# A gated attention / gMLP decoder layer: 18 projection column tiles, taken in pairs, by a seven-product scheme over two thirds of the tokens

## The reference, cut to what matters

```python
h = _rmsnorm(x, g_mp)
z = h @ w_in                    # columns: q | k | v (768 each) | u (512) | v_sg (512) | gate_a | gate_b
o_a, rows = core(q, k, v)       # dilated window attention, 3 groups x 4 heads; rows: k and v to keep
vs = _layernorm(jax.nn.gelu(vs), lvg, lvb)
o_b = jax.nn.gelu(u) * _spatial_mix(vs, w_sg, b_sg)      # chunks of 128 tokens
m = jax.nn.sigmoid(ga) * (o_a @ w_pa) + jax.nn.sigmoid(gb) * (o_b @ w_pb)
x = x + _rmsnorm(m @ w_o, g_mq)
h = _rmsnorm(x, g_fp)
x = x + _rmsnorm((jax.nn.silu(h @ w_g) * (h @ w_u)) @ w_d, g_fq)
```

## Time and profile before

| | |
|---|---|
| median of 3 runs | 1502.27 us (1501.37 to 1504.39) |
| span of the profiled execution | 1499.6 us, its own time is not listed apart |
| PE busy | 1480.6 us, 99% of the span |
| DVE, ACT, POOL busy | 49%, 40%, 14% |
| granted PE clock | 0.997 of full speed over the span |
| DMA | 147 MB, 98 GB/s in the mean |

### The profile page before, as it was taken

How to read it: one execution, slowest core, us unless ns; L and a number is a source line. 1 busy time by engine, 2 the same in 40 slices (tenths; PEclk the granted TensorE clock), 3 DMA queues, 4 the chain that set the end, 5 groups by cost and what they waited for, 6 DMA issues and landing times.

```text
span 1499.6 us, 26632 instructions
## 1 busy us (share of the span) xinstructions
PE 1480.6 (99%) x11001; PEld 1433.9 (96%) x11001; DVE 733.7 (49%) x1328; ACT 595.6 (40%) x1183; POOL 216.0 (14%) x225
## 2 busy tenths in 40 slices
PE   7999999999999999999999999999999999999998
PEld 6999999999999999997789999999999999999997
DVE  6104552242213437474678857655755683225323
ACT  6215553443224522245586333333333363235322
POOL 2000000000000026150003224222422210002000
PEclk9999999999999999999999999999999999999999
DMA  5111113111112127125644222232232474446341
GB/s 198 47 52 43 43 30 103 29 30 32 53 43 75 30 85 211 46 86 171 231 128 145 71 86 92 72 100 85 79 99 86 138 243 132 114 111 196 113 141 58
DMA packets 186666, 147.09 MB, mean 98 GB/s; under 512 B 7003, under 2 KB 168803, under 8 KB 186549
## 3 DMA queue, kind: packets, MB, share of 16 engines
q1 hardware_dynamic: 182656, 133.31, 29.6%
q0 software_dynamic: 2720, 7.89, 1.8%
q10 hardware_dynamic: 1172, 4.23, 0.7%
HBM read 121.84 MB, written 23.58 MB: 97 GB/s over the span
## 4 chain that ended last, share of the span: by engine, by line
PE 91%; DVE 4%; DMA 2%; ACT 1%; issue 1%; POOL 0%; DVEq 0%; ACTq 0%
PE bank L787 9%; PE bank L789 8%; PE bank L788 8%; PE bank L1357 6%; PE bank L1358 6%; PE bank L1359 6%; PE psAB L1285 3%; PE bank L1285 3%; PE psAB L1287 3%; PE psAB L1286 3%; PE bank L1286 3%; PE bank L1287 3%; PE bankC L787 3%; PE bankC L789 3%; PE bankC L788 3%; PE psT L783 3%
## 5 line engine op out<-in xcount | busy, mean ns | idle before, releaser
L787 PE MATMUL bank<-h_hi,w_hi 128*128 128x344 f32 x752 | 248.6, 331 | 2.7 <-DVE h_lo L2001 2.2
L789 PE MATMUL bank<-h_hi,w_lo 128*128 128x344 f32 x752 | 240.8, 320 | 0.0
L788 PE MATMUL bank<-h_lo,w_hi 128*128 128x344 f32 x752 | 240.5, 320 | 0.0
L1357 PE MATMUL bank<-a_hi,s_hi 128*128 128x258 f32 x704 | 200.2, 284 | 0.2 <-DVE s_lo L2442 0.2
L1358 PE MATMUL bank<-a_lo,s_hi 128*128 128x258 f32 x704 | 198.7, 282 | 0.0
L1359 PE MATMUL bank<-a_hi,s_lo 128*128 128x258 f32 x704 | 198.7, 282 | 0.0
L1988 DVE TENSOR_TENSOR w_lo<-w_raw,w_hi 128x1024 fp32r<-128x1024 f32 x71 | 87.5, 1233 | 203.5 <-ACT w_hi L1398 141.7
L787 PEld LDWEIGHTS bank<-h_hi,w_hi 128*128 128x128 f32 x752 | 142.0, 189 | 7.2 <-issue 3.5
L788 PEld LDWEIGHTS bank<-h_lo,w_hi 128*128 128x128 f32 x752 | 141.9, 189 | 0.0
L789 PEld LDWEIGHTS bank<-h_hi,w_lo 128*128 128x128 f32 x752 | 141.8, 189 | 0.0
L1357 PEld LDWEIGHTS bank<-a_hi,s_hi 128*128 128x128 f32 x704 | 133.0, 189 | 0.6 <-issue 0.5
(11 more groups left out here) (527 smaller groups left out, 3672.6 us busy)
## 6 DMA issues: line engine op xcount, KB each, us to landing
rawd<-in_w_down SPq DMA_DIRECT2D x32, 704.0 KB, 6.5
w_raw<-in_w_in SPq DMA_DIRECT2D x42, 512.0 KB, 3.9
raw<-in_w_gate SPq DMA_DIRECT2D x26, 512.0 KB, 4.1
raw<-in_w_up SPq DMA_DIRECT2D x26, 512.0 KB, 5.3
w_raw<-in_w_out SPq DMA_DIRECT2D x24, 512.0 KB, 3.7
a_raw<-a_rows SPq DMA_DIRECT2D x20, 516.0 KB, 6.2
a_rows<-ab SPq DMA_DIRECT2D x18, 516.0 KB, 2.7
xin<-in_x_prompt SPq DMA_DIRECT2D x8, 512.0 KB, 7.5
```

The source lines that it names most:

```text
L787: mm(out[:, 0:TG], w_hi[par][:, ws], hi[:, k, tgc[tg]], start=first, stop=False)
L788: mm(out[:, 0:TG], w_hi[par][:, ws], lo[:, k, tgc[tg]], start=False, stop=False)
L789: return mm(out[:, 0:TG], w_lo[par][:, ws], hi[:, k, tgc[tg]], start=False, stop=last)
L1357: mm(out, hi[:, k, :], xh[:, k, :], start=(kg == 0 and k == 0), stop=False)
```

## The change

Eighteen of the 26 column tiles of u, v_sg, q, k, v are no longer made as units. Nine *steps* (`SX = 9`) each make two column tiles `e = 0, 1`. Steps 0 to 2 make six tiles of u and v_sg; steps 3 to 8 make the twelve tiles of k and v, those of both head pairs. The two tiles and the two halves of the 1024 input channels form a 2x2 block of weights, and token groups 0 and 1 with the two channel halves form a 2x2 block of activations; their product is made with seven half-depth products (`A11`, `S2`, `A12`, `S3`, `S1`, `A22`, `S4`) in place of eight. Token group 2 is made plainly (`t0` to `t3`). Each is 4 chunks x 3 = 12 matmuls of 344 columns, so a step is 132 matmuls. The two remaining `uv` units stay, and q stays: stages `q0` and `q1` have 3 units each.

Around it:

- **Sums of activations**, once, before step 0: S1, S2, S4 on DVE (seven operations of 128x1376), S3 on POOL (three), and a split of each (ACT, DVE).
- **Sums of weights**: four POOL operations of 128x512 in each step.
- **Splits**: eight slots of 128x512 for each step, four buffered. Slot q + 4 is split once PE is done with slot q, which reads the place that q + 4 takes.
- **Copies out**: four by ACT and five sums by DVE (`u2`, `u3`, `C22`, `C21`, `C12`, 128x344) in each step; PE goes on in a bank after its copy or sum.
- **DRAM**: the k and v tiles go through `stage` to `kv_rows`, six transfers for each step, and are loaded back before their use, pair 0 after the last step and pair 1 in `gb0` and `q1`.
- **The chain of a chunk** is now tied to slots. With i the slot number counted from step 3, chunk c is turned after slot 5c, its statistics stand at 5c + 1, square root, scaling and the next Gelus at 5c + 2, mixing after slot 5c + 3, gating at 5c + 4.
- The `merge` of pair 0 and the turns of pair 1's k and v stand beside 3 units of `q1` in place of 9.

```diff
-STAGES = [("uv", 8, 8), ("qkv0", 9, 9), ("pb", 4, 8), ("gb0", 4, 4), ("qkv1", 9, 9), ("gb1", 4, 4),
+STAGES = [("uv", 2, 2), ("q0", 3, 3), ("pb", 4, 8), ("gb0", 4, 4), ("q1", 3, 3), ("gb1", 4, 4),
+SX = 9
+SX_UV = 3
+SX_TILES = [(0, 6), (0, 7), (0, 8), (0, 3), (0, 4), (0, 5), (1, 4), (1, 5), (1, 3), (1, 6), (1, 7), (1, 8)]
+SX_GROUPS = (("A11", "t0"), ("S2",), ("A12", "t1"), ("S3",), ("t2",), ("S1",), ("A22",), ("S4", "t3"))
+SX_SLOTS = 4
...
@@ tensor
+            def sx_group(s, o, name):
...
+                if s == 0:
+                    if name == "A11":
+                        pe.wait_ge(free[2], 2)
...
+                    if name[0] == "S":
+                        pe.wait_ge(x_lo, 9 + ("S2", "S1", "S3", "S4").index(name) + 1)
...
+                if name == "A12":
+                    pe.wait_ge(lu_s, sx_act(s, "p1"))
+                elif name in ("S3", "A22", "S4"):
+                    pe.wait_ge(sum_s, sx_dve(s, {"S3": "u2", "A22": "u3", "S4": "C22"}[name]))
...
+                for k in range(4):
+                    mm(out, hi[:, k, :], xh[:, k, :], start=(begin and k == 0), stop=False, skip_group_check=True)
+                    mm(out, hi[:, k, :], xl[:, k, :], start=False, stop=False, skip_group_check=True)
+                    ins = mm(out, lo[:, k, :], xh[:, k, :], start=False, stop=(k == 3), skip_group_check=True)
+                ins.then_inc(pe_ev, 1)
...
-            for j in range(9):
-                u, m = U0["qkv0"] + j, M0["qkv0"] + j
-
-                def after(b, tg, j=j):
-                    if tg == 0:
-                        ln_turn(j)
-                    if tg == 2:
-                        ln_mixing(j)
-                unit(u, m, u % 2, 8, h_hi, h_lo, after=after)
+            for s in range(SX):
+                for o in range(8):
+                    pe.wait_ge(sp_lo, 8 * s + o + 1)
+                    for name in SX_GROUPS[o]:
+                        sx_group(s, o, name)
+                    if s >= SX_UV:
+                        c, phase = divmod(8 * (s - SX_UV) + o, 5)
+                        if c < 9 and phase == 0:
+                            ln_turn(c)
+                        elif c < 9 and phase == 3:
+                            ln_mixing(c)
+            pe.wait_ge(lu_s, sx_act(SX - 1, "P1"))
+            pe.wait_ge(sum_s, sx_dve(SX - 1, "C12"))
@@ scalar
+            def sx_high(q):
...
+                if q >= SX_SLOTS:
+                    act.wait_ge(pe_ev, sx_used(q - SX_SLOTS))
...
+                fn(sx_hi[q % SX_SLOTS][:, :, :], sx_source(q), ACT.Copy).then_inc(sp_hi, 1)
...
+                    if s >= SX_UV and c < 9 and phase == 2:
+                        ln_root(c)
+                    sx_high(8 * s + o + SX_SLOTS)
+                    if o == 2:
+                        sx_copy(s, "P0")
+                    elif o == 7:
+                        sx_copy(s, "P1")
@@ vector
+            for name in ("S1", "S2", "S4"):
+                sa_sum(name)
+            sa_low(0, "S2")
+            sx_low(0)
+            sx_low(1)
+            sa_low(1, "S1")
+            sx_low(2)
+            sx_low(3)
+            sa_low(2, "S3")
+            sa_low(3, "S4")
...
+            for s in range(SX):
+                for o in range(8):
+                    if o in (1, 3, 5, 6):
+                        sx_sum(s, {1: "u2", 3: "u3", 5: "C22", 6: "C21"}[o])
+                    sx_low(8 * s + o + SX_SLOTS)
+                    if o == 7:
+                        sx_sum(s, "C12")
+                    if s >= SX_UV:
+                        c, phase = divmod(8 * (s - SX_UV) + o, 5)
+                        if phase == 0 and 1 <= c <= 9:
+                            ob_low(c - 1)
+                        elif c < 9 and phase == 1:
+                            ln_stats(c)
+                        elif c < 9 and phase == 2:
+                            ln_scale(c)
+                        elif c < 9 and phase == 4:
+                            ln_gate(c)
@@ gpsimd
+            sx_weights(0)
+            sa_third()
...
+            sx_in_place(0)
+            for s in range(1, SX):
+                sx_weights(s)
+                sx_in_place(s)
```

More of the change, by code:

```diff
@@ L53, with sx_done, sx_used, sx_act @@
 UNITS, JOBS = _u, _m
+SX = 9
[3 more added lines that the diff above has]
+SX_SLOTS = 4
+SX_SPLITS = 8 * SX
+SX_SUMS, SX_COPIES, SX_EVENTS = 5 * SX, 4 * SX, 11 * SX
+SX_ACT_STEPS = [(s, e) for s in range(SX_UV, SX) for e in range(2)]
+SX_OUT = (64 * (SX - SX_UV), 32 * (SX - SX_UV))
+A_BEFORE = (96, 224, 0, 0, 0, 0)
+SX_FLAT = [x for group in SX_GROUPS for x in group]
+def sx_done(s, what):
+    return len(SX_FLAT) * s + SX_FLAT.index(what) + 1
+def sx_used(q):
+    return sx_done(q // 8, SX_GROUPS[q % 8][-1])
+def sx_act(s, what):
+    return 4 * s + ("p1", "C11", "P0", "P1").index(what) + 1
+def sx_dve(s, what):
+    return 5 * s + ("u2", "u3", "C22", "C21", "C12").index(what) + 1
+def sx_tile(s, e):
+    return 2 * (s - SX_UV) + e
+def sx_by_residue(s):
+    return s >= SX_UV and SX_TILES[sx_tile(s, 0)][1] in (1, 2, 4, 5)
 ORDER = (0, 1, 2, 3, 8, 4, 5, 6, 7)
@@ L865, in kv_turns @@
             def kv_turns(pair, places):
-                last = max(min(p // 2 + 6, 8) for p in places)
-                for tg in range(3):
-                    pe.wait_ge(free[tg], M0[f"qkv{pair}"] + last + 2)
+                pe.wait_ge(a_in[0], 48 * (pair + 1))
+                if max(places) >= 6:
+                    pe.wait_ge(a_in[1], 112 * (pair + 1))
                 if pair:
@@ new lines, in sx_sum @@
+            def sx_sum(s, what):
+                group, e, tg, other = {"u2": ("S2", 1, 0, "p1"), "u3": ("S3", 1, 1, "p1"), "C22": ("S1", 1, 1, "u3"),
+                                       "C21": ("A22", 0, 1, "p1"), "C12": ("S4", 1, 0, "u2")}[what]
+                dve.wait_ge(pe_ev, sx_done(s, group))
+                if other == "p1":
+                    dve.wait_ge(lu_s, sx_act(s, "p1"))
+                else:
+                    dve.wait_ge(sum_s, sx_dve(s, other))
+                if what == "C21":
+                    dve.wait_ge(sum_s, sx_dve(s, "u3"))
+                if s > SX_UV and what in ("u2", "u3"):
+                    late = (e, tg) == (1, 0)
+                    dve.wait_ge(a_out[late], (64, 32)[late] * (s - SX_UV))
+                place = sx_to(s, e, tg)
+                in1 = sx_to(s, 0, 1) if other == "p1" else place
+                v.tensor_tensor(place, sx_from(s, sx_bank(group), tg), in1, ALU.add).then_inc(sum_s, 1)
```

439 lines of the change are left out of this document (332 added, 107 removed).

## The result

The changed kernel took **1527.85 us** (median of four runs, 1524.71 to 1530.97), the kernel before 1502.86 beside it (1501.37 to 1504.39): the ratio is 1.0168, with a 95% interval of 1.0150 to 1.0187. It is slower, as forecast; the forecast was 1522 in a range of 1507 to 1530. The profiled execution took 1529.73, with a span of 1527.9; that is 1.9 above the median, and the spans of the two profiled executions lie 28.3 us apart where the medians lie 25.0 apart. One execution of the kernel before, beside e5 to e8, took 1593.45 us at a granted clock of 0.849 and is left out of all comparisons, which makes the median there 1501.8.

What follows compares the result with a forecast made beforehand. PE, busy for 99% of the span, was taken to bound the kernel. Saved matmuls (-17.0) against waits and low clock at the start, in the chunks and at step 8 gave +20.0 us, from 1502.3 to 1522, range 1507 to 1530.

Steps and rivals of the forecast that it cites:

- The gain: Product matmuls on PE: 1188 in place of 1296, 108 fewer at 0.157 us each, -17.0 us.
- The start of step 0: PE waits for slot 0's low half on DVE, which takes turns with POOL, until 57.4: +10.3 us.
- The clock behind it: After the wait at step 0's start, one stretch of PE at a low clock: +1.4 us (0 to 2.8).
- The first step: In step 0 PE waits at S3 for DVE's low halves, splits and u2: +2.5 us (0 to 4.1).
- First turn: The first chunk's turn waits for a Gelu behind ACT's copy and a table load: +0.8 us.
- Nine chunks: PE waits at each layer norm chunk's mixing for statistics, root and scaling: +19.5 us in all.
- POOL's lock in them: POOL's weight sums hold up DVE's scaling in chunks 1, 2 and 4: +1.5 us (0 to 4).
- Clock in the chunks: Forecast none; as rival, the clock falls after each chunk's wait, nine times 1.4 us more, 1535 us; chance 6%.
- At nothing: Other sums and copies, spills, reloads, weight loads and merge were taken to cost PE nothing.
- rival without turns (1509): DVE and POOL don't hold each other up at the start: +2.3 in place of +10.3, 1509 us; chance 12%.
- rival that the layer norm doesn't reach PE: DVE's scaling ends within PE's next slot, so no chunk waits: 1500 us, or 1489 with a short start; chance 7%.
- rival of a late spill: C12's spill lands late, so DVE stands at u2, 1 to 2 us in five steps: 1530 us; chance 5%.

Runs made afterwards that it cites:

- e5: Changed kernel with its start laid out anew in the order PE wants, S3 made on DVE in two passes, POOL's early weight sums later: 1521.09 us.
- e8: Changed kernel with POOL's weight sums cut to 2 of 128 columns from step 3 on, so part of the computation is left out: 1526.84 us.
- e7: Changed kernel with e5's start, e3's later mixing, and DVE's statistics and scaling ahead of the slot's low half: 1489.88 us, ratio 0.9915 to the kernel before.
- e1: Changed kernel with POOL's three passes for the sum S3 moved to DVE: 1523.84 us.
- e11: e9 plus 66 unread matmuls ahead of the first seven-product matmul, in a free bank so that they fill PE's wait there: 1522.83 us.
- e9: Changed kernel with 114 matmuls that nobody reads put into the nine chunk waits ahead of the mixing: 1521.59 us.
- e2: Changed kernel with the first weight tile's high and low halves made ahead of the sums of x, order only: 1528.68 us.
- e3: Changed kernel with each layer norm chunk mixed one slot later on PE; gate, high and low half follow: 1505.52 us.
- e4: Changed kernel with the edits of e1, e2 and e3 together: 1510.4 us.

## Why the prediction was right, and where it was not

The direction, the range and the mechanism held: the saving is whole, and waits at the start and in the nine chunks take more than it gives. Of the 25.0 us by which the medians differ the sum had 20.0. That 1527.85 still lies within a range that ends at 1530 is in part luck: one of the four runs took 1530.97, and with the half clock that e5 shows, 12.2 us outside the waits in place of 8.3, the median would be near 1532 (an estimate from these two traces). By the terms, against the profiled execution:

| term | predicted | shown |
|---|---|---|
| The gain | -17.0 | -17.0 in the account, confirmed by e7 to about 1 us |
| The start of step 0 | +10.3 | +11.7, of them 8.7 the turns with POOL (e1) |
| The clock behind it | +1.4 | +2.7; no stretch low in e11 |
| The first step (`S3`) | +2.5 | 0; hidden by the half clock, 2.1 when PE is at full clock (e11) |
| First turn | +0.8 | +0.6 |
| Nine chunks | +19.5 | +18.9 with the next line |
| POOL's lock in them | +1.5 | 2.1 of the 18.9 (e8) |
| Clock in the chunks | 0, nine times 1.4 as a rival of 6% | +8.5, at four of nine waits (e9: gone when filled) |
| The end of step 8 | +1.0 | +0.7 |
| At nothing | 0 | nothing that the profile names; with all unnamed, 2.0 |

The step that failed is **The clock behind it**, with the rival that went with it. The forecast took one low stretch at the start and none in the chunks, because no stretch of the trace of before had repeated waits, and gave the other case 6% as an all or nothing: nine stretches or none. Four of the nine waits had one, and by the windows they cost 1.7, 1.7, 1.7 and 3.4 us, not 1.4 each; the long one stands at the longest wait, 3.42 (but in e5 also at waits of 2.63 and 2.84, and in e8 the wait of 3.42 cost 1.7). The mark is 28.1 us late where the sum said 20.0: 8.5 of clock in the chunks, less 2.4 by which the other terms together were too high, and the 2.0 without a name.

**The clock behind it** and **The first step** were also added as if they stood apart. The wait at `S3` was reckoned from a PE that arrives at 66.8 at full clock, while the term before had just made PE later by the half clock. The runs show the one covering the other: in the changed kernel, with half clock at the start, PE does not wait at `S3`; without it, and with all else the same, PE waits 2.11 (e11). The two terms together were +3.9 and measured +2.7.

The rule quoted from the Trainium skill, "TensorE: Matmul & The Clock Gate", section "HAM oscillation — how this bites in real kernels", that waits bring the clock down tile after tile, is borne out in kind (e9) and not in every tile.

The start was right in its mechanism and 1.4 short. I had given DVE's turns between POOL's passes to two sums of x. In the trace the two mask operations take the first two turns, each waiting for a whole pass of POOL to do 0.3 us of work (2.80 and 3.15). When POOL ended, DVE had one of its sums done and not two, and one more of 1.6 us was left. That POOL ended at 46.86 all the same (forecast 47.1) is two errors that cancel: POOL waited for one sum and not two, and its first pass began 1.1 us later, at 35.83 for 34.7. The whole start is late there, as the first jobs are (they start at 31.14, before at 30.11), 0.25 us of it from the first matmul of the trace on; DVE's scaling of x at 26.56 took 1.83 beside POOL's first weight sums, where it took 1.28 before. The rival without turns (1509) falls with e1, and so does its start of +2.3 as a description of the changed kernel; it describes e1, where PE went on at 50.20.

The chunks with POOL's part came to 18.9 for 21.0 (19.5 + 1.5), and without it to 16.8 (e8) for 19.5. In the order 0 to 8 the waits are 2.02, 0.48, 2.79, 1.48, 1.57, 2.62, 1.97, 2.53 and 3.42, forecast 2.35, 0.85, 3.1, 1.2, 1.2, 3.1, 2.35, 3.1 and 3.8, in which POOL has no part. So seven of the nine were put too high, by 0.3 to 0.6, and chunks 3 and 4 only look close: without POOL's sums they are 0.65 each. The rival that the layer norm doesn't reach PE falls with them. Its reckoning does stand: e7, with all waits far under the 14.0 us that it named, is faster than before. The rival of a late spill falls too: PE waits for no reloaded tile, and DVE's `u2` isn't late in steps 4 to 8.

Open is which of the waits the clock answers. The changed kernel and e1 have the same nine waits to within 0.05 us each, and the clock fell at chunks 0, 2, 7 and 8 in one and at 5, 7 and 8 in the other, as in e2; in e5 and e8, at five. In these five traces it fell at 20 of the 26 chunk waits of 2.0 us and more, and at none of the 19 shorter ones (in e3 and e4 it fell at one of 1.53). I could not forecast the 8.5 us for a single run from the waits, and the spread of the four runs of the changed kernel (6.3 us, at mean clocks from 0.984 to 0.990) is of the same size.
